# An expert's bias row: 32 copies written by the DMA engines, or one written and copied by VectorE

## What is computed

```
gu = xb @ w_gu[e] + b_gu[e]                 # xb: a block of rows of one expert
x_glu = minimum(gu[:, 0::2], 7)
x_lin = clip(gu[:, 1::2], -7, 7)
act = x_glu * sigmoid(1.702 * x_glu) * (x_lin + 1)
y = act @ w_dn[e] + b_dn[e]                 # then weighted by the router and added to the row
```

## Time and profile before

| | us |
|---|---|
| median of 3 runs | 2314.43 (2310.81 to 2315.14) |
| profiled execution, time | 2316.25 |
| profiled execution, span from first to last instruction | 2314.4 |
| TensorE busy | 2200.6 |
| VectorE busy | 1029.5 |
| GpSimd busy | 849.1 |
| ScalarE busy | 333.1 |

### The profile page before, as it was taken

One profiled execution on the slowest core, in us unless ns is written; L12 is line 12 of the kernel. 1 busy time (PEld: TensorE's weight loads), 2 busy tenths in 40 slices (PEclk: granted clock), 3 DMA queues, 4 the chain that ended last, 5 costly groups with the idle time before them and its releaser, 6 DMA issues.

```text
span 2314.4 us, 80327 instructions
## 1 busy us (share of the span) xinstructions
PE 2200.6 (95%) x31685; PEld 1502.2 (65%) x31685; DVE 1029.5 (44%) x3487; ACT 333.1 (14%) x919; POOL 849.1 (37%) x1658
## 2 busy tenths in 40 slices
PE   6999989999899899999999999999999999999995
PEld 2777776666544467777777777767675567775573
DVE  2464237777255434343434343434443344443344
ACT  0000017777211000000000000000000000000001
POOL 2011006554224443434343434344443344443433
PEclk9999998999999999999999999999999999999998
DMA  9531051000336787686768686878979978989996
GB/s 312 191 137 58 12 158 35 1 2 1 116 107 229 275 289 250 218 282 224 274 220 287 215 286 213 289 253 276 380 250 355 377 272 317 381 305 390 390 379 224
DMA packets 183488, 534.03 MB, mean 231 GB/s; under 512 B 30152, under 2 KB 59216, under 8 KB 183248
## 3 DMA queue, kind: packets, MB, share of 16 engines
q1 hardware_dynamic: 143472, 479.09, 55.7%
q0 software_dynamic: 33360, 39.96, 8.2%
q10 hardware_dynamic: 6480, 12.72, 1.9%
HBM read 498.27 MB, written 33.34 MB: 230 GB/s over the span
## 4 chain that ended last, share of the span: by engine, by line
PE 55%; DMA 14%; issue 2%; SPq 1%; POOL 1%; DVE 1%; POOLq 0%; another core or an unknown queue 0%; ACT 0%; DVEq 0%; ACTq 0%
PE psum L1701 34%; PE psum L1713 17%; DMA w_ring<-in_w_gate_up 8%; DMA w_ring<-in_w_down 4%; PE psum L1259 4%; DMA x_gathered<-h_rows,scalars_i 1%; SPq L1583 0%; DVE x L1399 0%; POOL slot_list L1214 0%; DMA x<-x_rows 0%; PE psum L1268 0%; DMA token<-k_pairs 0%; SPq L1145 0%; DMA x_rows<-y_out,scalars_i 0%; SPq L1608 0%
## 5 line engine op out<-in xcount | busy, mean ns | idle before, releaser
L1701 PE MATMUL psum<-w_ring,xT 128*32 128x320 f32 (+1 forms) x18304 | 1023.7, 381 | 19.2 <-issue 14.7
L1701 PEld LDWEIGHTS psum<-w_ring,xT 128*32 128x32 f32 x18304 | 696.6, 110 | 340.7 <-issue 41.5
L1713 PE MATMUL psum<-w_ring,actT 128*32 128x256 f32 x9152 | 531.0, 382 | 17.3 <-DMA w_ring<-in_w_down 15.7
L1713 PEld LDWEIGHTS psum<-w_ring,actT 128*32 128x32 f32 x9152 | 349.8, 111 | 152.6 <-DMA w_ring<-in_w_down 20.7
L1642 POOL TENSOR_TENSOR scalars<-scalars 128x1 f32<-128x1 f32 x575 | 108.9, 189 | 728.8 <-DVE xT L1768 562.6
L1754 DVE TENSOR_TENSOR glu<-psum,expert_bias 128x160 f32<-128x160 f32 (+1 forms) x286 | 83.1, 291 | 537.8 <-PE psum L1701 537.7
L1748 ACT ACTIVATE glu<-glu 128x160 f32<-128x160 f32 (+1 forms) x286 | 88.7, 310 | 1444.3 <-DVE glu L1756 1429.7
L1659 POOL DMA_INDIRECT x_rows<-y_out,scalars_i x142 | 228.0, 1606 | 47.2 <-issue 46.9
L783 POOL TENSOR_SCALAR scores<-scores,coef 128x64 f32<-128x64 f32 (+5 forms) x128 | 134.1, 1063 | 137.5 <-DVE coef L992 137.5
L1650 POOL DMA_INDIRECT x_gathered<-h_rows,scalars_i x144 | 153.3, 1064 | 81.3 <-issue 79.2
L1776 DVE TENSOR_TENSOR psum<-psum,expert_bias 128x256 f32<-128x256 f32 x143 | 61.8, 432 | 242.2 <-PE psum L1713 223.4
(11 more groups left out here) (246 smaller groups left out, 1882.7 us busy)
## 6 DMA issues: line engine op xcount, KB each, us to landing
w_ring<-in_w_gate_up SPq DMA_DIRECT2D x128, 1280.0 KB
w_ring<-in_w_down SPq DMA_DIRECT2D x128, 1024.0 KB
w_ring<-in_w_gate_up SPq DMA_DIRECT2D x128, 768.0 KB
ada_then_cmp_in<-in_w_ada SPq DMA_DIRECT2D x16, 1024.0 KB, 6.3
expert_bias<-bias_by_quarter ACTq DMA_DIRECT2D x128, 96.0 KB
ada<-in_w_ada SPq DMA_DIRECT2D x8, 1024.0 KB, 5.6
xt<-in_x SPq DMA_DIRECT2D x8, 512.0 KB, 6.3
w_uv_then_w_out<-in_w_in SPq DMA_DIRECT2D x4, 1024.0 KB, 9.5
```

Source lines behind the costliest of these rows:

```text
L1701: last = nc.tensor.matmul(psU[h][j * BLK:(j + 1) * BLK, :], xT[:, k, :], w[:, j], start=(k == 0), stop=(k == KD - 1))
L1713: last = nc.tensor.matmul(psO[m * BLK:(m + 1) * BLK, :], actT[h][:, i, :], w[:, m * Q:(m + 1) * Q], start=(k == 0), stop=(k == KD - 1))
```

## The change

The four loads of an expert's bias move one row each, into the first partition of a group of 32. Before the bias is used, VectorE runs a shuffle within each group whose mask is 0 for all 32 partitions, so that every partition gets what the first one holds. The semaphore `s_bias` counts 64 for the four loads and 1 for the shuffle. The wait at the head of every segment becomes a call of `spread_bias` at the head of those segments in which a new expert begins (31; not of the second halves). The first expert's shuffle stands ahead of `assign(TILES - 2, 0)`, where its wait stood further down, ahead of the first `gates`. GpSimd's `clear` sets both bias tiles to zero first.

```diff
@@ route, VectorE
         tiles(dve, body)
+        parts.spread_bias(dve, 0)
         assign(TILES - 2, 0)
...
-        dve.wait_ge(parts.s_bias[0], 64)
         parts.gates(dve, 0, 0, 0)
@@ clear, GpSimd
-        pool.wait_ge(s_clear, 3)
+        for i in range(2):
+            nc.gpsimd.memset(b_e[i][:], 0.0).then_inc(s_clear, 1)
+        pool.wait_ge(s_clear, 5)
@@ load_bias, ScalarE
         for q in range(4):
-            act.dma_start(b_e[at][q * BLK:(q + 1) * BLK, :], rows[q].partition_broadcast(BLK)
-                          ).then_inc(s_bias[at], 16)
+            act.dma_start(b_e[at][q * BLK:q * BLK + 1, :], rows[q:q + 1, :]).then_inc(s_bias[at], 16)
+
+    def spread_bias(dve, p):
+
+        at = HALF_OF[p]
+        turn = sum(HALF_OF[q] == at for q in range(p + 1))
+        dve.wait_ge(s_bias[at], 65 * turn - 1)
+        nc.vector.stream_shuffle(b_e[at][:], b_e[at][:], mask=[0] * BLK).then_inc(s_bias[at], 1)
+        dve.wait_ge(s_bias[at], 65 * turn)
@@ expert_gates, VectorE
-        e = SEGMENTS[g][0]
+        e, part = SEGMENTS[g]
         at = HALF_OF[e]
-        dve.wait_ge(parts.s_bias[at], 64 * sum(HALF_OF[p] == at for p in range(e + 1)))
+        if g and part != 1:
+            parts.spread_bias(dve, e)
```

## The result

| | us |
|---|---|
| kernel before, median of 5 runs | 2313.62 (2310.81 to 2315.14) |
| changed kernel, median of 5 runs | 2291.05 (2288.88 to 2294.09) |
| ratio | 0.9903, 95% interval 0.9892 to 0.9914 |
| span of the profiled execution, before and after | 2314.4 and 2288.7 |

The change makes the kernel 22.6 us faster.

What follows compares the result with a forecast made beforehand. TensorE, 95% busy, was taken as the bound, except for 15.7 us of weight waits where DMA engines are full. Gains of 8.0 + 0.2 + 2.7 + 0.3 = 11.2 us off 2314.43 gave 2303.2 us, range 2299 to 2312.5.

Steps and rivals of the forecast that it cites:

- The price of a load: DMA time that removing one expert's bias broadcast frees for the weights: 0.69 to 1.35 us, taken as 1.0.
- Eight loads in the chains: Eight bias loads lie in the DMA chains ahead of TensorE's weight waits: 8.0 us gained, 5.5 to 10.8 by the bounds.
- A: TensorE's weight waits at 1748.48 and 1751.41 us, 3.29 us together; two of the eight loads counted there.
- B: TensorE's weight waits at 1827.18 and 1829.70 us, 3.86 us together; two of the eight loads counted there.
- C and D: Five weight waits between 2085.72 and 2159.80 us, 8.34 us together, sharing one DMA stream; four of the eight loads.
- the end: TensorE's last weight wait, 0.22 us, expected to vanish; counted as 0.2 us.
- The clock behind B: TensorE's granted clock, 0.82 in the up product after B, would stay 1.00 with shorter waits: 2.7 us gained.
- The head: First expert: its old load runs beside a gather VectorE waits 0.59 us for; gain 0 to 0.6, taken 0.3 us.
- The shuffle: About 1.0 us on VectorE at 31 changes of expert, hidden in at least 2.52 us of idle time: cost 0.
- One engine carrying the rows: Rival: one DMA engine carries the rows and the clock still falls behind B: 5.7 us gained, 2308.7; within own case's 0.78.
- Waits set by issue rather than engine time: Rival: SyncE's issuing limits the weights, so freed DMA time stays unused: 2313 to 2315 us, no change; chance 0.14.
- The late shuffle: Rival: shuffle exceeds VectorE's idle cover at switches; at 4 us each, 2349 us; chance 0.08 together with a late bias landing.

Runs made afterwards that it cites:

- experiment 3: Weight stream from expert 27 to 31, with four bias loads, read off the profiles: 143.4 us in the kernel before, 135.5 in the changed kernel; five kernels vary the load.
- chains_only: Kernel before with single-row loads and shuffle for only eight of 32 experts, at places 18 to 21 and 26 to 29: 2294.08 us, ratio 0.991.
- first_two: Kernel before with single-row loads and shuffle for only the first two experts: 2310.52 us, ratio 0.9979.
- tiny_copy: Changed kernel with the shuffle replaced by a copy of one column onto itself, biases left unspread: 2292.62 us, ratio 0.9916.

## Why the prediction was right or wrong, step by step

**The price of a load: the step that failed.** "Net 0.69 to 1.35 us per expert; I take 1.0." It measures 2.0 us (experiment 3), above the upper bound. The bound took the time of q10's own packets as all that the load takes from the engines. It left out that the other queue's packets get slower beside it, 0.7 us per load. A row that pointed there was at hand: the engines moved 365 GB/s in that window and 397 to 399 in the stretches of the earlier trace rows.

**Eight loads in the chains: right** (chains_only). With 2.0 us each, the terms read: A is capped at its own 3.3 us, since only 3.29 us of waits stood there; B at 3.9, plus the clock's 2.7; C and D 4 x 1.97 = 7.9; the end 0.2. The sum is 18.0; the profiles show 17.9 from block 3 on, and 20.6 against the second profile of the kernel before. "Every wait is larger than what is taken from it" fell with the price: at A and B nothing is left to wait for.

**The clock behind B: right in size, by a sign that does not hold.** 1.00 where it was 0.82, 7.0 us gained at B where the terms above make 6.6. But the prediction argued that B's waits would be shorter than A's 3.29 us, which "cost no clock". In the second profile of the same kernel 2.99 us at A did cost some (1.93 for 1.07, 7.70 for 7.09). What made the term safe was that nothing was left to wait for at B, and that followed from the price that the prediction had too low: luck. Behind C the clock holds as well, and gives about 2.9 us there (7.09 for 9.08, 1.07 for 1.94). As the prediction argued, it is no gain of its own: D's weights come by the same stream, and C and D together gain 7.2 us, close to what four loads free.

**The head: mis-sized.** 0 to 0.6 us, taken 0.3; it measures 2.5 to 7.2 us (first_two). The prediction followed VectorE's 0.59 us wait and did not ask what the first expert's weights, still landing then, gain: the eighth piece lands some 2 to 3 us sooner. Whether that makes up the 4.6 stays open.

**The shuffle, the memsets, the end: right.** 1044 ns against 1.0 us, 763 ns against at most 1.0, both hidden. The rows of the transposes bounded the shuffle well. The cover of 2.52 us proved thinner in use: 0.40 us is left at the tightest switch.

**The rivals.** One engine carrying the rows: one packet and so one engine for each row, no cost found. Waits set by issue rather than engine time: refuted, the waits went with the load. The late shuffle: appears only with three of them. The sum on record, with 2.0 in place of 1.0 and caps at A and B (18.0), and 4.6 for 0.3, is 22.6 us, what was measured; that it fits so closely is luck within these intervals.

## What to carry to other kernels

Where one queue keeps the DMA engines full, price a small transfer on another queue by what the full queue moves less while it runs, not by the small queue's own packet time: here 2.0 us against 1.35. Halving its bytes may buy nothing as long as it stays several transfers spread thin over all engines; one transfer in place of four bought half of the price here, single rows spread on chip by an idle engine all of it. And ask of every wait on TensorE that goes away whether the clock behind it then holds, which was worth 2.7 us at B; a wait that only gets shorter is no promise of that, and a slower product gives nothing back where another path is longer.

## What the runs showed of the hardware

- Four 96 KB transfers cost the weight stream 2.0 us, one of 393 KB 0.9 us, four of 48 KB still 1.9, four single rows about nothing. (2.0 less a fourth of what a kernel saves in the stretch from expert 27 to 31; the changed kernel's price is taken as nothing.)
- A 5120-byte packet of the weight queue took 198 ns ahead of a load, 256 beside four broadcasts of 32 rows, 302 beside those of 16 rows, 205 beside one transfer of 128 rows.
- A shuffle of 128x768 fp32 within groups of 32 took 1044 ns and 14 ns for its mask, against 403 ns for a transpose of 256 elements: 1.36 ns per element and 1.57.
- A wait of 2.41 us before a product went with a granted clock of 0.72 in it, one of 1.73 us with 1.00 in the changed kernel and with 0.73 in tiny_copy. At A two waits of 1.43 and 1.86 us cost no clock in one execution, and 1.53 and 1.46 us did in another of the same kernel. So the wait's length alone does not tell.
